# Feature-major ends, a root on ScalarE and a third buffer for the split activations in a four-layer decoder trunk

## The reference

```
x = x + W_out( mixer( rms_norm(x, gain) ) * silu(gate) )      # each layer
mixer: layer 0 retention, 1 differential attention, 2 RG-LRU, 3 retention
rms_norm(x) = x * rsqrt(mean(x*x over the features) + 1e-6) * gain
```

## Time and profile before

| what | value |
|---|---|
| median of 3 runs | 3680.82 us (3678.0 to 3686.5) |
| the profiled execution | 3687.29 us, span 3685.5 us |
| mean granted TensorE clock | 0.945 |
| PE / DVE / ACT / POOL busy | 89% / 40% / 32% / 20% |

### The profile page before, as it was taken

How to read it: one execution, slowest core, us unless ns; L and a number is a source line. 1 busy time by engine, 2 the same in 40 slices (tenths; PEclk the granted TensorE clock), 3 DMA queues, 4 the chain that set the end, 5 groups by cost and what they waited for, 6 DMA issues and landing times.

```text
span 3685.5 us, 56759 instructions
## 1 busy us (share of the span) xinstructions
PE 3283.7 (89%) x20193; PEld 2945.7 (80%) x20193; DVE 1456.4 (40%) x3286; ACT 1192.5 (32%) x2294; POOL 749.5 (20%) x476
## 2 busy tenths in 40 slices
PE   4999999997996999999968799969799999999788
PEld 3979798886996777777747688859697979798688
DVE  4161514235234334344434566642515161514431
ACT  4232313223123444444432344531323232323211
POOL 3101111113333111110003322233311202011341
PEclk7999999997998999999987899979899999999799
DMA  3647465557212444444443012131124242424611
GB/s 110 226 141 253 141 229 164 198 183 236 90 43 71 128 130 131 130 133 136 136 134 119 18 57 73 56 105 39 39 87 142 86 139 86 129 91 129 226 60 68
DMA packets 512941, 450.90 MB, mean 122 GB/s; under 512 B 24598, under 2 KB 460598, under 8 KB 510674
## 3 DMA queue, kind: packets, MB, share of 16 engines
q1 hardware_dynamic: 406294, 325.75, 29.0%
q10 hardware_dynamic: 106428, 122.27, 9.9%
HBM read 348.56 MB, written 166.50 MB: 140 GB/s over the span
## 4 chain that ended last, share of the span: by engine, by line
PE 70%; DVE 11%; issue 6%; ACT 5%; POOL 4%; DMA 3%; SPq 1%; ACTq 0%; DVEq 0%; POOLq 0%
PE psum L266 17%; PE psum L267 17%; PE psum L268 17%; PE psum L861 3%; POOL Hl L291 3%; PE psum L857 3%; DVE hraw L367 2%; PE psum L1254 2%; ACT Hh L288 2%; PE psum L1227 2%; DMA arena<-scratch_kc 2%; PE psum L853 1%; DVE hraw L328 1%; PE psum L836 1%; PE psum L869 1%
## 5 line engine op out<-in xcount | busy, mean ns | idle before, releaser
L266 PE MATMUL psum<-Hh,Wh 128*128 128x384 f32 (+1 forms) x4896 | 1663.1, 340 | 185.4 <-POOL Hl L291 75.8
L267 PE MATMUL psum<-Hl,Wh 128*128 128x384 f32 (+1 forms) x4896 | 1602.4, 327 | 0.0
L268 PE MATMUL psum<-Hh,Wl 128*128 128x384 f32 (+1 forms) x4896 | 1601.4, 327 | 0.0
L266 PEld LDWEIGHTS psum<-Hh,Wh 128*128 128x128 f32 x4896 | 952.3, 195 | 242.6 <-issue 101.9
L242 POOL TENSOR_TENSOR Wl<-wraw,Wh 128x1024 fp32r<-128x1024 f32 (+1 forms) x208 | 495.2, 2381 | 2388.7 <-ACT Wh L238 2388.7
L267 PEld LDWEIGHTS psum<-Hl,Wh 128*128 128x128 f32 x4896 | 955.2, 195 | 13.9 <-issue 8.2
L268 PEld LDWEIGHTS psum<-Hh,Wl 128*128 128x128 f32 x4896 | 952.1, 194 | 0.0
L238 ACT ACTIVATE Wh<-wraw 128x1024 fp32r<-128x1024 f32 (+1 forms) x208 | 216.1, 1039 | 312.9 <-PE psum L268 224.1
L291 POOL TENSOR_TENSOR Hl<-hraw,Hh 128x384 fp32r<-128x384 f32 (+1 forms) x252 | 226.1, 919 | 327.5 <-ACT Hh L288 327.5
L376 DVE TENSOR_TENSOR xT<-psum,xT 128x384 f32<-128x384 f32 x168 | 86.3, 514 | 370.3 <-PE psum L268 369.8
L288 ACT ACTIVATE Hh<-hraw 128x384 fp32r<-128x384 f32 (+1 forms) x252 | 116.2, 488 | 261.2 <-DVE hraw L367 125.4
(11 more groups left out here) (216 smaller groups left out, 3183.0 us busy)
## 6 DMA issues: line engine op xcount, KB each, us to landing
wraw<-in_ret_w_in SPq DMA_DIRECT2D x96, 512.0 KB, 3.9
scratch_kc<-in_cache_kt SPq DMA_DIRECT2D x64, 512.0 KB, 6.3
scratch_vc<-in_cache_v SPq DMA_DIRECT2D x64, 512.0 KB, 7.0
arena<-in_state_ret ACTq DMA_DIRECT2D x64, 512.0 KB, 6.0
out_ret_state_sample<-arena ACTq DMA_DIRECT2D x64, 512.0 KB, 2.8
arena<-scratch_kc SPq DMA_DIRECT2D x64, 512.0 KB, 5.2
arena<-scratch_vc SPq DMA_DIRECT2D x64, 512.0 KB, 5.4
scratch_on<-arena ACTq DMA_DIRECT2D x80, 256.0 KB, 3.4
```

What stands on the lines that cost most here:

```text
L266: nc.tensor.matmul(out, hi, xh, start=(k == 0), stop=False)
L267: nc.tensor.matmul(out, hi, xl, start=False, stop=False)
L268: last = nc.tensor.matmul(out, lo, xh, start=False, stop=(k == kt - 1))
```

## The change

1. The host hands over `x_cols`, the tokens already feature-major, and the gains already per partition, and takes `y_cols` feature-major. The turning at both ends goes, with its PSUM copies, and so does DVE's sum of squares at the start: PE adds eight squared tiles with eight matmuls against `ones`. Each finished feature tile of the last layer is stored straight from `xT`.
2. In all layer norms the square root and DVE's reciprocal become Ln and Exp(-0.5 x) on ScalarE, with one table set loaded ahead at chunk 0.
3. `hraw` gets a third buffer (`HR = 3`): DVE waits for POOL's tile n-3.

```
+HR = 3
-        hraw = sb("hraw", [P, 2, WMAX])
+        hraw = sb("hraw", [P, HR, WMAX])
...
-            act.activation(rst[:, 0:w], NB[:, 0:w], ACT.Sqrt, bias=eps_t[:, 0:1], scale=1.0 / D_MODEL)\
-               .then_inc(nrm_sq, 1)
+            if c == 0:
+                act.preload_act_table_set("natural_log_exp_and_others")
+            act.activation(rst[:, 0:w], NB[:, 0:w], ACT.Ln, bias=eps_t[:, 0:1], scale=1.0 / D_MODEL).then_inc(nrm_ln, 1)
+            act.wait_ge(nrm_ln, n + 1)
+            act.activation(rst[:, 0:w], rst[:, 0:w], ACT.Exp, scale=-0.5).then_inc(nrm_sq, 1)
...
-            ch.link(nc.vector.reciprocal(rst[:, 0:w], rst[:, 0:w]))
...
-                if n >= 2:
-                    dve.wait_ge(h_lo, n - 1)
-                nc.vector.scalar_tensor_tensor(hraw[:, n % 2, 0:w], ...
+                if n >= HR:
+                    dve.wait_ge(h_lo, n - HR + 1)
+                nc.vector.scalar_tensor_tensor(hraw[:, n % HR, 0:w], ...
...
         def input_sp(sp):
+            for c in range(NC_):
+                c0, w = CHUNKS[c]
+                for half in range(2):
+                    k0 = 4 * half
+                    src = A["x_cols"][k0 * P:(k0 + 4) * P, c0:c0 + w].rearrange("(k p) t -> p k t", p=P)
+                    sp.dma_start(xT[:, k0:k0 + 4, c0:c0 + w], src).then_inc(xin_ld[2 * c + half], 16)
+                if c == 0:
+                    load_w(sp, Pos(0), 0, w_block(A["ret_w_in"][0], 0, KT, RQK))
...
         def input_pe(pe):
+            for c in range(NC_):
+                c0, w = CHUNKS[c]
+                if c:
+                    pe.wait_ge(nrm_sq, c)
+                for k in range(KT):
+                    pe.wait_ge(sq_done, KT * c + k + 1)
+                    last = nc.tensor.matmul(NB[:, 0:w], ones[:, :], sqb0[:, k, 0:w], start=(k == 0), stop=(k == KT - 1))
+                last.then_inc(nrm_ps, 1)
...
         def input_act(act):
             for c in range(NC_):
                 c0, w = CHUNKS[c]
+                if c:
+                    act.wait_ge(nrm_ps, c)
                 for k in range(KT):
+                    if k % 4 == 0:
+                        act.wait_ge(xin_ld[2 * c + k // 4], 16)
+                    act.activation(sqb0[:, k, 0:w], xT[:, k, c0:c0 + w], ACT.Square).then_inc(sq_done, 1)
                 if c:
                     norm_act(act, 0, c - 1)
...
+            def sp_(sp):
+                for k in range(KT):
+                    for c0, w, c in [(0, T, NC_ - 1)] if k < KT - 1 else [(*CHUNKS[c], c) for c in range(NC_)]:
+                        sp.wait_ge(unit_ev, ev_val(q_end - KT + k, c))
+                        sp.dma_start(A["y_cols"][k * P:(k + 1) * P, c0:c0 + w], xT[:, k, c0:c0 + w]).then_inc(y_st, 16)
+                sp.wait_ge(y_st, 16 * (KT - 1 + NC_))
```

More of the change, by code:

```diff
@@ L390, in trunk @@
         al = arena()
[L391 to L398, removed]
+        sqb0 = al.take(KT, WMAX)
+        xin_ld = sems("xin_ld", 2 * NC_)
         def input_sp(sp):
             sp.sem_inc(raw_free, CR)
-            sp.dma_start(ident[:, :], A["c_ident"]).then_inc(const_ld, 16)
-            sp.dma_start(ngr[0:32, :], A["norm_g"].rearrange("l (k p) -> (l k) p", p=P)).then_inc(const_ld, 16)
@@ L411, in input_sp @@
                     load_w(sp, Pos(0), 0, w_block(A["ret_w_in"][0], 0, KT, RQK))
-        def input_blocks(c):
-            return [(0, 1, 2), (3, 4, 5), (6, 7, 8)][c]
+                    sp.dma_start(ng[:, :, :].rearrange("p l k -> p (l k)"), A["norm_gp"]).then_inc(const_ld, 16)
+                    sp.dma_start(ident[:, :], A["c_ident"]).then_inc(const_ld, 16)
         def input_pe(pe):
-            pe.wait_ge(const_ld, 32)
[L419 to L434, removed]
@@ L480, in input_dve @@
[L480 to L518, removed]
-                    nc.vector.tensor_copy(*evac(b, 1)).then_inc(y_d, 1)
-            def sp_(sp):
-                for b in range(NBLK + 1):
-                    sp.wait_ge(y_a, b + 1)
-                    sp.wait_ge(y_d, b + 1)
-                    dst = A["y_prompt"][0, b * P:(b + 1) * P, :] if b < NBLK else A["y_sample"][:, 0, :]
-                    sp.dma_start(dst, yo[0:P if b < NBLK else NS, b % 2, :]).then_inc(y_st[b % 2], 16)
-                sp.wait_ge(y_st[0], 16 * 5)
-                sp.wait_ge(y_st[1], 16 * 4)
-            return pe_, act_, dve_, sp_
@@ L1938, in _ @@
             sp.sem_inc(unit_ev, CR)
+            sp.sem_inc(ss_done, KT * NC_)
             input_sp(sp)
@@ L2013 @@
     arrays, A = {}, {}
-    laid = {name: value for name, value in inputs.items() if name != "cache_k"}
+    laid = {name: value for name, value in inputs.items() if name not in ("cache_k", "x_prompt", "x_sample", "norm_g")}
+    xs = _np.concatenate([_np.asarray(inputs["x_prompt"])[0], _np.asarray(inputs["x_sample"])[:, 0]], axis=0)
+    laid["x_cols"] = _np.transpose(xs)
+    laid["norm_gp"] = _np.transpose(_np.asarray(inputs["norm_g"]).reshape(4, KT, P), (2, 0, 1)).reshape(P, 4 * KT)
     laid["cache_kt"] = _np.transpose(_np.asarray(inputs["cache_k"]), (0, 1, 3, 4, 2))
```

77 lines of the change are left out of this document (25 added, 52 removed).

## The result

The changed kernel takes 3573.69 us (median of 4 runs, 3571.11 to 3576.05), the kernel before, measured beside it, 3682.14 (4 runs, 3678.0 to 3686.5): a ratio of 0.9705, 95% interval 0.9688 to 0.9722. The profiled executions' spans are 3685.5 and 3574.3, a difference of 111.2.

A forecast was written before the change was run, and what follows sets the result against it. The end of DVE's and POOL's chain was taken to set every fill's time. Third buffer 45.7, root 13.2, start 14.4 and end 15.2 sum to 88.5 us off 3680.8, giving 3592; 8-in-10 range 3576 to 3623.

The forecast's parts named there:

- Third buffer, turns: Fills 1 to 10: DVE and POOL alternate, 1.28 us a tile against 1.50, saving 45.7 us; chance 0.60.
- Bursts: Rival, fills: the port's holder runs on, 1.39 to 1.42 a tile; buffer saves 18 to 29; 3609 to 3622; chance 0.20.
- the third buffer gives nothing: Rival, fills: each instruction locks the other engine out for its whole duration; kernel at 3640 us; chance 0.06.
- Root: Norms in fills 3, 5, 8: Ln and Exp replace root and reciprocal, saving 4.4 us each, 13.2 together.
- Start: Kernel start to the first turning of keys: 14.4 us earlier, at 69 in place of 83.18; bounds 9 to 19.
- the clock gives back more: Rival, fills: denser PE work raises the granted clock sooner, 5 to 20 us more saved; 3572 to 3587; chance 0.09.
- End: After the last residual: direct feature-major stores leave 2.5 us in place of 17.7, saving 15.2 (14 to 15.5).

The follow-up runs named there:

- experiment one: The changed kernel with two `hraw` buffers in place of three (HR = 2): 3623.19 us, ratio 0.9836 to the kernel before.
- ten: The kernel before with only the third `hraw` buffer added (HR = 3): 3631.36 us, ratio 0.9858 to the kernel before.
- experiment seven: The changed kernel with the root's result in PSUM in place of SBUF: 3550.06 us, ratio 0.964 to the kernel before.
- experiment four: The changed kernel with 69 waiting instructions ahead on TensorE's queue, putting its loops at their old place in a code block: 3586.45 us, ratio 0.9735.
- five: The kernel before with 187 waiting instructions ahead on TensorE's queue, meant to give its loop the changed kernel's place: 3681.36 us, ratio 0.9997.
- Eleven: The changed kernel with 49 waiting instructions ahead on TensorE's queue: 3580.40 us, ratio 0.9717 to the kernel before.
- eight: The changed kernel with 69 instructions ahead on TensorE's queue and layer 0's page copies kept off the head borders: 3586.73 us, ratio 0.974.
- experiment six: The changed kernel with 153 waiting instructions ahead on TensorE's queue: 3602.78 us, ratio 0.9783 to the kernel before.

## Why the forecast missed

**Third buffer, turns.** Right. The two engines take turns at 1.28 a tile, as worked out from 0.41 behind the release and 0.86 for POOL. For fills 1 to 10, 45.7 were forecast; they lose 49.1 when it is taken back (experiment one) and gain 46.9 when it comes alone (ten). Fill 0's 4.0 come on top; the sum had 2.5 for them under the start, although it priced the same eight tiles a chunk at 3.9 in the other norms. *Bursts* and *the third buffer gives nothing* are refuted by the rows and by experiments one and ten. (By its own 18 us the upper end of *bursts* is 3620, not 3622; nothing hangs on it.) As to the lock itself: experiment seven shows that it hangs on DVE's second SBUF operand. The Trainium skill (SBUF — State Buffer, "Who interferes with whom") names that pair, and the trace agrees: 1072 against 613 ns. That the lock is "held for the full instruction" ("Terms") would make a tile 1.6 us, and 1.28 is measured.

**Root.** Priced at 4.4 a norm, it is worth 4.9 with two buffers and 5.8 with three, since less covers the second and third reciprocal. The sum priced the two edits one after the other, with the waits of the old fill. That the norms came out at 25.2 against 25.0 is luck: from the start of the root to the end of the fill the three are 27.5 shorter (fill 3: 39.7 before, 30.7 after), but in the changed kernel the root starts later behind the fill before it, 1.7 of it ahead of fill 8.

**Start: the first term that was mis-sized, and its path was wrong.** 14.4 was taken, 20.0 measured, just past the upper bound of 19. By the experiments 11.0 of it are the ends, 4.9 to 6.1 the root and 2.9 to 4.2 the buffer, according to which of the two comes first; with the buffer last, ends and root give 17.1, where the sum had 11.9.

The prediction let the turning follow PE's first two chunks, at 7.7 us each, to 68.8. It follows the fill. In every run the first turning stands 1.8 to 2.1 us behind the end of fill 0, before as after (81.41 to 83.18, 61.11 to 63.15); ScalarE makes the last chunk's copies, loads a table, copies a weight block, and only then takes out the result that the turning waits for:

```profile
59.85 0.42 ACT L289 ACTIVATE Hh<-hraw 128x264 fp32r<-128x264 f32 x1 [0.47 <-DVE hraw L330]
60.29 1.28 ACT L239 ACT_TABLE_LOAD   x1
61.58 1.06 ACT L239 ACTIVATE Wh<-wraw 128x1024 fp32r<-128x1024 f32 x1
62.54 0.85 ACT L830 ACTIVATE arena<-psum 128x384 f32<-128x384 f32 x2
```

The row for the old turning names the same wait, 5.70 us for ACT. With the prediction's own end of the fill, 65, the turning would have been put at 67. PE did run those two chunks at the high level, from 48.07 to 58.1, but then stood idle for 5.04 us, so their price changed nothing:

```profile
48.00:58.00 10.00, 8.99 (x50) 8.40 (x49) 7.77 (x10) 4.82 (x11) 9.17 (x10) 1.00 0.24 93
```

The other 3.9 us are the fill's own end, 61.1 in place of 65. There PE's eight sums of a 384-wide chunk, priced at 1.3 to 1.48 each, took 7.85 and 7.79 us, 0.98 each. Over the second chunk's sums the windows view shows why:

```profile
28.30:32.90 4.60, 4.57 (x7) 2.53 (x8) 3.59 (x5) 2.09 (x4) 3.22 (x3) 0.50 0.00 0
33.30:36.10 2.80, 2.80 (x9) 1.33 (x7) 2.80 (x4) 1.05 (x2) 2.80 (x3) 1.00 0.00 0
```

At a granted clock of 0.50 a pass takes 0.65 us, as priced (a sum is two passes), and at 1.00 0.31; the clock rose halfway. (Over the first chunk's sums the view prints 1.00 throughout, but its passes show the same two paces, seven in 4.57 us and then nine in 2.78.) ScalarE's squares took 0.43 each, not 0.5. The first tile stands at 28.42, not 30.9, and the root of chunk 1 starts at 41.33, not 46.3. The rival *the clock gives back more* named the sign, but put it into the fills; there it did little (fill 1 at 0.69 in place of 0.56, the fill's length set by DVE and POOL all the same).

**The term that was missing.** The forecast counted what instructions cost, not where they stand. The heads of layers 0 and 3 stood in the sum with nothing, and no reason was given. The new ends remove 69 instructions ahead of the retention loop in TensorE's program, the loop's start moves away from the end of a fetched block, and three pauses of 1.6 to 3.4 us, with what follows each, disappear. Experiments four and five give the size: 7.4 of layer 0's 11.8 come back with the old place, and 10.5 go in the kernel before with the new one. Eleven and the packets' times give the mechanism, eight excludes the transfers. The 4.5 of layer 3 are not pauses: none stands there before or after. There the mean granted clock is 0.98 before and 0.99 after, and 2.6 of the 4.5 come back in experiment four; what sets the clock there stays open. The groups of the waits on "issue" in front of TensorE's first matmul of a tile had it in plain sight, before and after (total us, times, longest):

```profile
PE psum L266 <- issue: 26.8, 12, 4.1
```

```profile
PE psum L267 <- issue: 16.8, 8, 2.8
```

I had read past such a row because no semaphore stands behind it. Three of the twelve are the pauses inside a chunk (7.8 us together); most of the others stand at the borders themselves, in both kernels.

**End.** Right: 15.9 against 15.2, the end 2.6 behind the last residual.

**What stays open.** The 3.8 us of layer 0 in experiment six and 4.0 in experiment eleven, which no pause explains; why the clock is low for longer in some kernels' heads; and the 5.0 us that the old root costs in the heads of layers 0 and 3.

## What to carry to other kernels

When two engines alternate on buffers, work out the turn first (what of each instruction can't overlap the other's), then count the buffers that let them reach it; and ask which operand makes them exclude each other, for moving the root into PSUM gave 23.6 us for three edited lines. Read the waits on "issue" on the engine that bounds the kernel: pauses after a fixed number of instructions behind a loop's start were code fetches here, and an edit anywhere ahead moved them, so a gain of a few tenths of a per cent may be the place and not the edit. Before a stretch is priced by one engine's work, look in the old trace which engine the row at its end waits for. Price a matmul at the start by both clock levels.

## What the runs showed of the hardware

- Instructions that only wait, put ahead of everything on TensorE's queue, changed the time by +6.7 us (49 of them), +12.8 (69) and +29 (153) of 3574. Of the 29, 3.8 lie at the start, where the waits themselves can count; most of the rest goes with the pauses and with the clock behind them.
- After the jump back to a loop's start, TensorE paused 0.7 to 3.6 us at the end of the first block of code, and went on 1.25 to 1.51 us after the second packet of 16,384 bytes had landed.
- An instruction on DVE that reads two SBUF tensors took 1072 ns on average beside POOL's work, and 613 ns with one of the two in PSUM; POOL's fell from 1220 to 1013.
- 187 instructions that only wait on a semaphore already reached held TensorE's first matmul until 21.36 us, where 9.62 is usual.
